# Rotary embedding on unnormalised queries in two sparse mixers, a new step order up to the first combinations, and later weight splits at three stage ends

## The chip, the cores and the metric

The kernel runs on one core of a Trainium2 chip. The metric is the device time of one execution in microseconds (us). All arithmetic is fp32: each large product is made of three TensorE passes over rounded high and low parts (w_hi·x_hi + w_hi·x_lo + w_lo·x_hi), so every weight tile has to be split into a high part (ScalarE, a copy) and a low part (VectorE, a subtraction) before TensorE can use it.

## What is computed

Two blocks of a transformer over 512 tokens and 1024 channels follow each other: four gated feed-forward layers around a retention/dilated mixer and a stick-breaking mixer (`first_block`), then two hybrid layers with a sparse mixer and a squared-ReLU feed-forward layer each (`second_block`). The change is mostly in the sparse mixer of the hybrid layers:

```python
def hybrid_layer(...):
    h = rms_norm_2(x, norm1) * (1.0 + scale1) + shift1
    proj = h @ w_in                      # u (pool), q, kv, gates
    y_pool = pool_mixer(u, pool_w, pool_scale)
    y_nsa = nsa_mixer(q, ..., gates, q_norm, k_norm, ...)
    x = x + gate1 * (jnp.concatenate([y_pool, y_nsa], axis=-1) @ w_out)
    ...                                  # feed-forward

def nsa_mixer(...):
    q = rope(rms_norm_2(q, q_norm), pos)             # 8 heads of 64
    s_c = einsum(q, k_cmp) * scale                   # compressed branch, 31 keys
    p_c = softmax(where(mask_c, s_c, NEG)); o_cmp = p_c @ v_cmp
    s = einsum(q, k_s) * scale; p = softmax(s)       # selected branch
    sw = einsum(q, k_w) * scale; pw = softmax(sw)    # window branch
    o = g0 * o_cmp + g1 * o_s + g2 * o_w
```

rms_norm divides each query head by a root mean square, one number for each token and head. rope is linear in q, so this factor can be applied to q itself or to the scores.

## The kernel before

The activation is kept as x[128, 8, 512]: channels on partitions, tokens along the free dimension. The program has ten stages, F1_0, HYB, F2_0, F1_1, STICK, F2_1, NSA_0, REL_0, NSA_1, REL_1. For each stage a planner (`plan_ffn`, `plan_hyb`, `plan_stick`, `plan_nsa`, `plan_rel`) writes one list of steps, and each of the five engine programs walks the same list in the same order and carries out its own part of each step. So where a step stands in the list sets its place in the queue of every engine that has a part in it. Between engines there are semaphores only (`wait_ge`).

Weights come in units of up to 128x1024 through a ring of four. The step ("load", u) makes ScalarE copy unit u to its high part `wh` (`weights` in `act_program`), makes VectorE subtract to the low part `wl` (`weights` in `dve_program`), and makes SyncE start the DMA of unit u+4 as soon as the low part of unit u has been written. A step that uses unit u is followed by the load of u+3 (AHEAD).

A sparse mixer (`plan_nsa`, stages NSA_0 and NSA_1) runs: normalisation; products for the compression window, the pooled groups 0 to 2, the keys and values; four q units ("q", 0..3: queries with tokens on partitions in PSUM banks 4 to 7); the gates unit; the pooled unit 3. Around them stand small steps:

- "q norm": ScalarE squares the four banks, VectorE sums over heads, ScalarE and VectorE form 1/rms (`root_means`, `norm_root`). It comes behind the gates unit.
- "q evac" t: VectorE multiplies bank 4+t by 1/rms, makes the two halves times sine and the whole times cosine in SBUF, GpSimd adds (semaphore `n_rot`). t = 0 and 1 stand before the pooled unit 3, t = 2 and 3 behind it.
- "turn q" t: TensorE transposes, ScalarE copies to qT.
- "u evac" 3, "u fine" 3, "pool" 3: GpSimd's running sums of the pooled group with window 16 (four doublings), VectorE's subtraction, one product, split into a0h and a0l slot 3.
- "cmp" n (n = 0, 1): scores of the compressed branch (16 small matmuls), mask and softmax on VectorE, ScalarE and GpSimd, all in one VectorE step, with waits for ScalarE and GpSimd inside it.
- "A" c (c = 0..7, a pair of heads and a branch, here called combination c): scores of 24 matmuls; VectorE `low_scores` (8 operations, scale, mask and maximum in one) and ScalarE 8 exponentials. "soft" c: reciprocal and gate on VectorE, eight multiplications on GpSimd. "B" c: 20 transposes of the weights, copied by ScalarE and VectorE. "C" c: product with the values. "pc": transposes of the compressed weights. Between them stand output products of 4 or 2 tiles ("out", with "load" and "add" to x).

In the loop over c (0 to 10) the steps are soft c-1, C c-3, B c-2, pc (only c = 2), outputs, A c. At c = 1, u fine 3, pool 3 and cmp 1 stand behind soft 0; at c = 0 there is A 0 alone, and cmp 0 is ahead of it.

At the end of a mixer stage, output unit d is followed by the add of d-1, the load of d+3 and the square of tile d-1 ("tile"). The loads behind the last three units belong to the next stage, 1024 columns wide. In NSA the next stage begins with a mean over all tiles, which waits for the last add; the transition's own first load comes ahead of it.

```python
for t in range(4):                     # "q norm" in dve_program, before
    dve.wait_ge(*n_sq[s, what, t])
    m = dve.tensor_reduce(v[:, n * t:n * t + n], src, AX.X, ALU.add)
```

## Time and profile before

| | us |
|---|---|
| median of 3 runs | 3204.42 (3203.95 to 3205.21) |
| the profiled execution, its own time | 3201.24 |
| its span, first to last instruction | 3199.4 |
| TensorE busy | 3091.9 |
| VectorE busy | 1673.5 |
| ScalarE busy | 1110.3 |
| GpSimd busy | 677.2 |

TensorE has work for 97% of the span. The mean clock granted to it is 0.981 of full speed. NSA_0 lies at about 2002 to 2235 us of the span, NSA_1 at about 2613 to 2846 us. A line of the profile names the kernel line of a helper (L68 is any matmul, L71 any transpose, L74 any ScalarE activation, L77 tensor_tensor, L80 scalar_tensor_tensor, L97 the scores' operation), so instructions are told apart by their tiles, shapes and order.

### The profile page before, as it was taken

Reading aid. Unit: us, or ns where it says so; the run is one execution under the profiler, and the core shown is the slowest. Engines: PE = TensorE matmul, PEld = TensorE weight load, DVE = VectorE, ACT = ScalarE, POOL = GpSimd, SP = SyncE. Lnnn points to the kernel's source line nnn. Section 1 sums busy time; section 2 is a strip of 40 time slices with the busy share of each in tenths; the row PEclk is TensorE's granted clock in tenths of the full one; section 3 lists DMA queues with packets and bytes.
Section 4 is the critical chain, followed back from the end, with each engine's and each line's share of the span. In section 5 each row is a group of like instructions: output and inputs, shape, how many; then the busy total and the mean of one; then the engine's idle time right before and its main releaser. Section 6 shows DMA issues by size and latency. Waiting matters only on the chain.

```text
span 3199.4 us, 36691 instructions
## 1 busy us (share of the span) xinstructions
PE 3091.9 (97%) x14506; PEld 2504.3 (78%) x14506; DVE 1673.5 (52%) x2485; ACT 1110.3 (35%) x1751; POOL 677.2 (21%) x543
## 2 busy tenths in 40 slices
PE   9999989999999999999999999978999997989999
PEld 7888877788888888877788887756888875768887
DVE  5455556644555454628754555666433356663333
ACT  4222334433223322334332224345422232543321
POOL 2100222111002100144111003255211123632110
PEclk9999999999999999999999999979999997999999
DMA  5344422343443344421243443202332330023332
GB/s 184 116 151 133 127 72 67 94 130 118 154 136 125 113 142 135 131 88 44 64 140 115 156 135 108 70 12 72 92 98 94 99 108 30 18 86 106 99 98 74
DMA packets 115802, 330.49 MB, mean 103 GB/s; under 512 B 13616, under 2 KB 18864, under 8 KB 115248
## 3 DMA queue, kind: packets, MB, share of 16 engines
q1 hardware_dynamic: 115632, 328.15, 32.5%
q8 instruction: 116, 1.90, 0.2%
q14 instruction: 54, 0.44, 0.0%
HBM read 326.00 MB, written 2.10 MB: 103 GB/s over the span
## 4 chain that ended last, share of the span: by engine, by line
PE 88%; DVE 5%; ACT 3%; POOL 2%; issue 1%; DMA 0%; SPq 0%; DVEq 0%; ACTq 0%; POOLq 0%
PE ps L68 87%; ACT s_tmp L74 2%; POOL s_tmp L85 2%; DVE s_tmp L77 1%; PE ps L71 1%; DVE s_wl L77 1%; DVE s_x L80 1%; POOL s_tmp L77 1%; DVE s_small L91 0%; DVE s_hl L80 0%; DVE s_tmp L80 0%; ACT s_hh L74 0%; ACT s_wh L74 0%; DVE s_tmp L100 0%; DVE s_tmp L97 0%
## 5 line engine op out<-in xcount | busy, mean ns | idle before, releaser
L74 ACT ACTIVATE s_wh<-s_raw 128x1024 fp32r<-128x1024 f32 (+3 forms) x562 | 544.5, 970 | 1134.6 <-PE ps L68 1133.5
L68 PE MATMUL ps<-s_hh,s_wh 128*128 128x512 f32 x2320 | 902.6, 394 | 23.4 <-ACT s_hh L74 12.3
L77 DVE TENSOR_TENSOR s_wl<-s_raw,s_wh 128x1024 fp32r<-128x1024 f32 (+3 forms) x535 | 606.8, 1135 | 556.6 <-ACT s_wh L74 556.2
L68 PE MATMUL ps<-s_hh,s_wl 128*128 128x512 f32 x2320 | 895.5, 391 | 0.4 <-DVE s_wl L77 0.3
L68 PE MATMUL ps<-s_hl,s_wh 128*128 128x512 f32 x2320 | 894.0, 390 | 0.2
L77 POOL TENSOR_TENSOR s_tmp<-s_tmp 128x512 f32<-128x512 f32 (+2 forms) x236 | 305.2, 1297 | 1714.1 <-ACT s_tmp L74 1472.6
L68 PEld LDWEIGHTS ps<-s_hh,s_wh 128*128 128x128 f32 x2320 | 437.4, 189 | 121.8 <-issue 12.0
L68 PEld LDWEIGHTS ps<-s_hl,s_wh 128*128 128x128 f32 x2320 | 437.6, 189 | 94.4 <-DVE s_hl L80 2.3
L68 PEld LDWEIGHTS ps<-s_hh,s_wl 128*128 128x128 f32 x2320 | 438.2, 189 | 93.2 <-DVE s_wl L77 1.8
L68 PE MATMUL ps<-s_a0h,s_wh 128*128 128x512 f32 x960 | 380.1, 396 | 7.4 <-ACT s_tmp L74 5.4
L68 PE MATMUL ps<-s_a0l,s_wh 128*128 128x512 f32 x960 | 376.5, 392 | 0.0
L68 PE MATMUL ps<-s_a0h,s_wl 128*128 128x512 f32 x960 | 376.4, 392 | 0.0
L68 PEld LDWEIGHTS ps<-s_a0h,s_wh 128*128 128x128 f32 x960 | 182.0, 190 | 46.6 <-ACT s_tmp L74 5.9
L68 PEld LDWEIGHTS ps<-s_a0h,s_wl 128*128 128x128 f32 x960 | 181.8, 189 | 38.5
L68 PEld LDWEIGHTS ps<-s_a0l,s_wh 128*128 128x128 f32 x960 | 182.1, 190 | 37.7 <-DVE s_a0l L77 0.3
L68 PE MATMUL ps<-s_a1h,s_wh 128*128 128x512 f32 x512 | 199.2, 389 | 0.0
L68 PE MATMUL ps<-s_a1l,s_wh 128*128 128x512 f32 x512 | 199.2, 389 | 0.0
L68 PE MATMUL ps<-s_a1h,s_wl 128*128 128x512 f32 x512 | 199.2, 389 | 0.0
L80 DVE SCALAR_TENSOR_TENSOR s_x<-ps,s_mod,s_x 128x512 f32<-128x512 f32 (+1 forms) x116 | 84.4, 730 | 202.7 <-PE ps L68 202.6
L74 ACT ACTIVATE s_tmp<-ps 128x512 f32<-128x512 f32 (+6 forms) x250 | 129.4, 546 | 107.8 <-PE ps L71 56.7
L85 POOL TENSOR_SCALAR s_tmp<-s_tmp,s_small 128x512 f32<-128x512 f32 (+3 forms) x128 | 137.7, 1098 | 64.5 <-DVE s_small L77 64.5
L80 DVE SCALAR_TENSOR_TENSOR s_x<-ps,s_x 128x512 f32<-128x512 f32 x129 | 88.2, 685 | 119.4 <-PE ps L68 119.4
(135 smaller groups left out, 2948.4 us busy)
## 6 DMA issues: line engine op xcount, KB each, us to landing
s_raw<-in_ff_dram SPq DMA_DIRECT2D x128, 512.0 KB, 3.6
s_tmp<-in_w_mod_dram SPq DMA_DIRECT2D x192, 256.0 KB, 3.6
s_raw<-in_f1i_dram SPq DMA_DIRECT2D x88, 512.0 KB, 3.6
s_raw<-in_f2i_dram SPq DMA_DIRECT2D x88, 512.0 KB, 3.6
s_raw<-in_f1o_dram SPq DMA_DIRECT2D x32, 512.0 KB, 3.6
s_raw<-in_f2o_dram SPq DMA_DIRECT2D x32, 512.0 KB, 3.6
s_raw<-in_nsa_dram SPq DMA_DIRECT2D x30, 512.0 KB, 3.6
s_raw<-in_hyb_dram SPq DMA_DIRECT2D x28, 512.0 KB, 3.5
```

The source lines that it names most:

```text
L68: return self.eng.matmul(o, w, m, **kw) if self.eng is not None else Blank()
L71: return self.eng.transpose(*a) if self.eng is not None else Blank()
L74: return self.eng.activation(o, a, f, **kw) if self.eng is not None else Blank()
L77: return self.eng.tensor_tensor(o, a, b, f) if self.eng is not None else Blank()
L80: return self.eng.scalar_tensor_tensor(o, a, s, b, f, g) if self.eng is not None else Blank()
L85: return self.eng.tensor_scalar(o, a, s, t, f) if g is None else self.eng.tensor_scalar(o, a, s, t, f, g)
```

## The change

1. `plan_nsa`: behind the fourth q unit come "q squares" and the four "q evac"; then the pooled unit 3 (ahead of the gates unit now, and the weights are laid out in that order); turn q 0 and 1; "q norm"; the gates unit; turn q 2 and 3; split 0; cmp 0; u fine 3; pool 3, all of that before A 0. The second half of the VectorE part of "cmp" n becomes a step of its own, "cmp p" n, at c = n+1. "pc" stands behind the outputs of c = 2.
2. "q evac" reads the raw queries in PSUM: two half products with sine, one with cosine. The product with 1/rms is gone. 1/rms times -0.125 is formed once (one more small operation) and is used as the per-partition scale in `low_scores`, where -0.125 stood. In "cmp" there are two further operations that multiply the scores by it.
3. In the NSA stages, the loads behind the last three output units come after the last add and tile; in HYB and STICK that holds for the last load only.

```diff
@@ plan_hyb and plan_stick
-        steps.append(("load", u + AHEAD))
+        if half == 0 or d < KT - 1:
+            steps.append(("load", u + AHEAD))
...
-    steps += [("add", 1, 7), ("tile", 7)]
+    steps += [("add", 1, 7), ("tile", 7), ("load", len(stream.src) - 1 + AHEAD)]
@@ plan_nsa
-    steps += [("turn kv", 2), ("turn kv", 3)]
+    steps += [("turn kv", 2), ("turn kv", 3), ("q squares",)] + [("q evac", t) for t in range(4)]
+    dense("pooled", 3)
+    steps += [("u evac", 3), ("turn q", 0), ("turn q", 1), ("q norm",)]
     dense("gates")
-    steps += [("gate row",), ("q norm",), ("q evac", 0), ("q evac", 1)]
-    dense("pooled", 3)
-    steps += [("gate turn",), ("u evac", 3), ("q evac", 2), ("q evac", 3)]
-    steps += [("turn q", t) for t in range(4)] + [("split", 0), ("cmp", 0)]
+    steps += [("gate row",), ("turn q", 2), ("turn q", 3), ("gate turn",), ("split", 0), ("cmp", 0), ("u fine", 3),
+              ("pool", 3)]
...
     for c in range(11):
+        if c in (1, 2):
+            steps.append(("cmp p", c - 1))
         if 1 <= c <= 8:
             steps.append(("soft", c - 1))
         if c == 1:
-            steps += [("u fine", 3), ("pool", 3), ("cmp", 1)]
+            steps.append(("cmp", 1))
...
-        if c == 2:
-            steps.append(("pc",))
         outs([halves.pop(0) for _ in range((0, 2, 2, 1, 1, 1, 1, 0, 0, 0, 0)[c])])
         outs([early.pop(0) for _ in range((0, 0, 0, 0, 0, 0, 0, 2, 2, 2, 2)[c])])
+        if c == 2:
+            steps.append(("pc",))
...
-        steps.append(("load", u + AHEAD))
+        if d + AHEAD < KT:
+            steps.append(("load", u + AHEAD))
+        else:
+            late.append(("load", u + AHEAD))
...
-    steps += [("add", KT - 1, 6), ("tile", KT - 1)]
+    steps += [("add", KT - 1, 6), ("tile", KT - 1)] + late
@@ act_program, nsa
+                    elif kind == "q squares":
+                        act.wait_ge(*unit[unit_at[s, "v", 1]])
+                        act.wait_ge(*n_rot[s, "kv", 3])
+                        for t in range(4):
+                            act.activation(S(38 + t), B(4 + t), ACT.Square).then_inc(*n_sq.up((s, "q", t)))
+                    elif kind == "q norm":
+                        norm_root(s, "q")
@@ dve_program, low_scores
-                                                 scale=-0.125, scalar=1e30, op0=ALU.add, op1=ALU.min,
+                                                 scale=scale(t, hd), scalar=1e30, op0=ALU.add, op1=ALU.min,
@@ dve_program, nsa, "q norm"
+                        if what == "q":
+                            dve.wait_ge(*n_new[s, "q", 2])
+                            dve.tensor_scalar(v, v, -0.125, None, ALU.mult).then_inc(*n_new.up((s, "q", 3)))
@@ "q evac"
-                        dve.wait_ge(*n_new[s, "q", 2])
-                        dve.tensor_tensor(n, heads(B(4 + t)), r.unsqueeze(2).to_broadcast([128, 8, 64]),
-                                          ALU.mult).then_inc(*n_nrm.up((s, "q", t)))
+                        q = heads(B(4 + t))
+                        dve.wait_ge(*n_sq[s, "q", t])
...
-                            m = dve.tensor_tensor(sn[:, :, 32 * h:32 * h + 32], n[:, :, 32 - 32 * h:64 - 32 * h], q_table(1, t, h),
-                                                  ALU.mult)
+                            dve.tensor_tensor(sn[:, :, 32 * h:32 * h + 32], q[:, :, 32 - 32 * h:64 - 32 * h], q_table(1, t, h),
+                                              ALU.mult)
-                        dve.tensor_tensor(n, n, q_table(0, t, None), ALU.mult).then_inc(*n_sn.up((s, "q", t)))
+                        dve.tensor_tensor(n, q, q_table(0, t, None), ALU.mult).then_inc(*n_sn.up((s, "q", t)))
@@ "cmp"
+                        for t in range(2):
+                            r = small_at("q", 0)[:, 16 * n + 8 * t:16 * n + 8 * t + 8].rearrange("p (i g) -> p g i", g=2)
+                            m = dve.tensor_tensor(p3[:, 8 * t:8 * t + 8, :].rearrange("p (g i) n -> p g i n", g=2),
+                                                  ps[:, 1, 256 * t:256 * t + 256].rearrange("p (g i n) -> p g i n", g=2, i=4),
+                                                  r.unsqueeze(3).to_broadcast([128, 2, 4, 32]), ALU.mult)
-                            m = dve.scalar_tensor_tensor(p3[:, 8 * t:8 * t + 8, :], B(b).rearrange("p (h n) -> p h n", n=32)[:, 8 * t:8 * t + 8, :],
-                                                         0.125, bc, ALU.mult, ALU.add)
+                            m = dve.scalar_tensor_tensor(p3[:, 8 * t:8 * t + 8, :], p3[:, 8 * t:8 * t + 8, :], -1.0, bc, ALU.mult,
+                                                         ALU.add)
```

## Rows read from the trace of the kernel before

**Rows 1.** The page's first part: busy time, share, instructions of each engine
```profile
PE 3091.9 (97%) x14506; PEld 2504.3 (78%) x14506; DVE 1673.5 (52%) x2485; ACT 1110.3 (35%) x1751; POOL 677.2 (21%) x543
```

**Rows 2.** Windows: start:end length, busy PE PEld DVE ACT POOL, granted clock, DMA share, GB/s
```profile
2061.10:2072.30 11.20, 11.20 (x52) 9.01 (x50) 5.03 (x12) 4.67 (x11) 0.00 (x0) 1.00 0.07 23
2072.30:2128.00 55.70, 30.73 (x156) 24.86 (x155) 36.71 (x83) 18.32 (x50) 23.57 (x25) 0.63 0.04 12
...
2135.30:2204.00 68.70, 65.64 (x480) 46.67 (x480) 43.65 (x143) 42.06 (x129) 52.39 (x49) 1.00 0.06 18
...
2684.00:2739.30 55.30, 30.30 (x154) 24.48 (x152) 36.39 (x83) 18.28 (x50) 23.52 (x25) 0.63 0.04 13
```

**Rows 3.** Windows of PE alone: length, busy PE, granted clock, DMA share, GB/s
```profile
2075.00:2115.00 40.00, 20.56 (x82) 0.50 0.02 7
```

**Rows 4.** Timeline of PE in NSA_0: start, us, operation, [idle before <-releaser]
```profile
2075.55 1.12 PE L71 MATMUL ps<-s_ident,s_tmp 128*128 128x128 f32 x4 [2.86 <-POOL s_tmp L77]
...
2089.81 3.65 PE L68 MATMUL ps<-s_tmp 128*128 128x64 f32 x16 [0.78 <-ACT s_tmp L74]
2093.39 3.89 PE L68 MATMUL ps<-s_tmpr 64*128 64x512 f32 x24
2106.37 5.35 PE L68 MATMUL ps<-s_tmp 128*128 128x512 f32 x18 [9.10 <-DVE s_tmp L80]
...
2127.97 0.50 PE L68 MATMUL ps<-s_a0h,s_wh 128*128 128x512 f32 x1 [2.70 <-ACT s_tmp L74]
2135.26 2.19 PE L68 MATMUL ps<-s_tmpr 64*128 64x512 f32 x24
```

**Rows 5.** Timeline of ACT and of DVE around q norm, q evac, u fine
```profile
2066.93 2.51 ACT L74 ACTIVATE s_tmp<-ps 32x512 f32<-32x512 f32 x5 [4.53 <-PE ps L68]
...
2068.03 2.46 DVE L91 TENSOR_REDUCE s_small<-s_tmp 128x8 f32<-128x512 f32 x4 [4.91 <-ACT s_tmp L74]
...
2072.67 1.49 DVE L77 TENSOR_TENSOR s_tmp<-s_tmp 128x256 f32<-128x256 f32 x3
...
2083.50 3.02 DVE L77 TENSOR_TENSOR s_tmp<-s_tmp 128x256 f32<-128x256 f32 x3
...
2105.14 1.08 DVE L80 SCALAR_TENSOR_TENSOR s_tmp<-s_tmp,s_ssum 128x496 f32<-128x496 f32 x1
```

**Rows 6.** Timeline of POOL: a q add, the u chain's first and last sum, soft 0
```profile
2074.24 1.26 POOL L77 TENSOR_TENSOR s_tmp<-s_tmp 128x512 f32<-128x512 f32 x1 [21.49 <-DVE s_tmp L77]
...
2078.52 1.03 POOL L77 TENSOR_TENSOR s_ssum<-s_ssum 128x511 f32<-128x511 f32 x1
...
2084.18 0.39 POOL L103 COPY s_tmp<-s_ssum 128x8 f32<-128x8 f32 x1
...
2105.01 8.52 POOL L85 TENSOR_SCALAR s_tmp<-s_tmp,s_small 128x512 f32<-128x512 f32 x8 [6.45 <-DVE s_small L77]
```

**Rows 7.** Groups of DVE by form, whole span: count | busy us, mean ns | idle before
```profile
L80 DVE SCALAR_TENSOR_TENSOR s_x<-ps,s_x 128x512 f32<-128x512 f32 x127 | 87.5, 689 | 117.7 <-PE ps L68 117.7
L80 DVE SCALAR_TENSOR_TENSOR s_x<-ps,s_mod,s_x 128x512 f32<-128x512 f32 x108 | 80.9, 749 | 195.0 <-PE ps L68 194.9
L97 DVE CUSTOM_DVE_ANT_0 s_tmp<-ps,s_tmp 128x512 f32<-128x512 f32 x40 | 26.0, 686 | 4.0 <-PE ps L68 3.8
```

**Rows 8.** Timeline at the end of NSA_0: DVE, ACT, PE
```profile
2223.10 1.66 DVE L77 TENSOR_TENSOR s_wl<-s_raw,s_wh 128x1024 fp32r<-128x1024 f32 x1
...
2228.11 1.04 ACT L74 ACTIVATE s_wh<-s_raw 128x1024 fp32r<-128x1024 f32 x1
2232.00 0.47 ACT L74 ACTIVATE s_tmp<-ps,s_eps 128x256 f32<-128x256 f32 x1 [2.85 <-PE ps L68]
...
2227.90 1.51 PE L68 MATMUL ps<-s_ssum,s_ones 128*128 128x256 f32 x4 [4.20 <-DVE s_x L80]
```

**Rows 9.** Timeline at the end of HYB: DVE, PE
```profile
637.04 1.21 DVE L77 TENSOR_TENSOR s_wl<-s_raw,s_wh 128x1024 fp32r<-128x1024 f32 x1
...
639.57 0.50 PE L68 MATMUL ps<-s_hh,s_wh 128*128 128x512 f32 x1 [1.92 <-DVE s_x L80]
```

More of the change, by code:

```diff
@@ L288, in out @@
             steps.append(("add",) + add)
-        steps.append(("load", u + AHEAD))
+        if half == 0 or d < KT - 1:
+            steps.append(("load", u + AHEAD))
         if half and d:
@@ L320, in plan_stick @@
         out(1, d, (1, d - 1) if d else None)
-    steps += [("add", 1, 7), ("tile", 7)]
+    steps += [("add", 1, 7), ("tile", 7), ("load", len(stream.src) - 1 + AHEAD)]
     return steps
@@ L384, in plan_nsa @@
             steps.append(("B", c - 2))
+        outs([halves.pop(0) for _ in range((0, 2, 2, 1, 1, 1, 1, 0, 0, 0, 0)[c])])
+        outs([early.pop(0) for _ in range((0, 0, 0, 0, 0, 0, 0, 2, 2, 2, 2)[c])])
         if c == 2:
             steps.append(("pc",))
-        outs([halves.pop(0) for _ in range((0, 2, 2, 1, 1, 1, 1, 0, 0, 0, 0)[c])])
-        outs([early.pop(0) for _ in range((0, 0, 0, 0, 0, 0, 0, 2, 2, 2, 2)[c])])
         if c < 8:
@@ L392, in plan_nsa @@
                 steps.append(("split", c // 2 + 1))
+    late = []
     for d in range(KT):
@@ L397, in plan_nsa @@
             steps.append(("add", d - 1, 6))
-        steps.append(("load", u + AHEAD))
+        if d + AHEAD < KT:
+            steps.append(("load", u + AHEAD))
+        else:
+            late.append(("load", u + AHEAD))
         if d:
             steps.append(("tile", d - 1))
-    steps += [("add", KT - 1, 6), ("tile", KT - 1)]
+    steps += [("add", KT - 1, 6), ("tile", KT - 1)] + late
     assert not halves and not early
@@ L1096, in nsa @@
                             for t in range(4):
-                                free[b0 + t] = [(n_nrm, (s, kind, t))] + ([(v_up, (s, 0, t))] if kind == "kv" else [])
+                                if kind == "kv":
+                                    free[b0 + t] = [(n_nrm, (s, "kv", t)), (v_up, (s, 0, t))]
+                                else:
+                                    free[b0 + t] = [(n_sn, (s, "q", t)), (n_sq, (s, "q", t))]
                     elif kind == "gates":
@@ L1535, in nsa @@
                         tile(s + 1, step[1])
-                    elif kind in ("kv norm", "q norm"):
-                        what = kind[:-5]
-                        act.wait_ge(*unit[unit_at[s, "v", int(what == "q")]])
+                    elif kind == "kv norm":
+                        act.wait_ge(*unit[unit_at[s, "v", 0]])
                         act.wait_ge(*win_add[s, 1, 1])
-                        n, b0, o = (256, 0, 0) if what == "kv" else (512, 4, 4)
                         for t in range(4):
-                            if what == "q" and t == 0:
-                                act.wait_ge(*h_lo[s, 7])
-                            dst = tmp[:, 42 + t, 0:n] if what == "kv" else S(46 + t)
-                            act.activation(dst, ps[:, b0 + t, 0:n], ACT.Square).then_inc(*n_sq.up((s, what, t)))
-                            if what == "kv":
-                                act.activation(vsw[:, t, :], ps[:, t, 256:512], ACT.Copy).then_inc(*v_up.up((s, 0, t)))
-                        norm_root(s, what)
+                            act.activation(tmp[:, 42 + t, 0:256], ps[:, t, 0:256], ACT.Square).then_inc(*n_sq.up((s, "kv", t)))
+                            act.activation(vsw[:, t, :], ps[:, t, 256:512], ACT.Copy).then_inc(*v_up.up((s, 0, t)))
+                        norm_root(s, "kv")
+                    elif kind == "q squares":
[5 more added lines that the diff above has]
+                        norm_root(s, "q")
                     elif kind == "turn kv":
@@ L1805, in mix_lo, with low_scores @@
                 dve.tensor_tensor(a0l[:, slot, :], src, f32(a0h[:, slot, :]), ALU.subtract).then_inc(*a_lo.up((s, 0, slot)))
-            def low_scores(s, i, g, z, st, bs, bias):
+            def low_scores(s, i, g, z, st, bs, bias, scale):
                 dve.wait_ge(*score[s, i, g])
@@ L1865, in hyb @@
                         for g in range(3):
-                            low_scores(s, i, g, Z[s][0], i % 2, ((6, 7), (4, 5), (2, 3))[g], DIL_BIAS)
+                            low_scores(s, i, g, Z[s][0], i % 2, ((6, 7), (4, 5), (2, 3))[g], DIL_BIAS,
+                                       lambda t, hd: -0.125)
                     elif kind == "soft":
@@ L2061, in nsa @@
                         for t in range(4):
-                            src = kv_tmp(t)[0] if what == "kv" else q_tmp(t)[0]
+                            src = kv_tmp(t)[0] if what == "kv" else heads(S(38 + t))
                             n = src.shape[1]
@@ L2197, in nsa @@
                         dve.tensor_tensor(p3, p3, mx.unsqueeze(2).to_broadcast([128, 16, 32]), ALU.subtract).then_inc(
-                            *cmp_low.up((s, n, 1)))
+                            *cmp_low.up((s, n, 2)))
+                    elif kind == "cmp p":
+                        n = step[1]
+                        p3 = S(36 + n).rearrange("p (h n) -> p h n", n=32)
+                        dn = small[:, 14 + n, :]
                         dve.wait_ge(*cmp_ex[s, n])
@@ L2434, in nsa @@
                             pool.tensor_copy(to[:, 0:sh], cur[:, 0:sh]).then_inc(*u_sum.up((s, g, n) if n < g else (s, g)))
-                    elif kind == "cmp":
+                    elif kind == "cmp p":
                         n = step[1]
```

28 lines of the change are left out of this document (14 added, 14 removed).

## The prediction

> **What bounds the kernel now.** I read the page first. TensorE is busy 3091.9 of 3199.4 us [rows 1], so all that can be won is its 107.5 us of idle time and what it loses at a low clock. Then I read the windows along the span. In NSA_0 the 55.7 us behind the pooled unit 3 hold only 30.7 us of TensorE work at a mean clock of 0.63; NSA_1 has the same hole, 55.3 us with 30.3 [rows 2]. The hole is 25 us of idle time plus a clock loss: from 2075 to 2115 the granted clock is 0.50 (1.2 GHz), with 20.56 us busy that would be 10.3 at 2.4 GHz [rows 3]. From 2135.3 to 2204 TensorE is busy 65.6 of 68.7 us at full clock [rows 2], so there is next to nothing to win there. Third I read the TensorE timeline for what it waits on. Turn q 0 waits 2.86 us for a GpSimd add, that is, for the q norm and evacuation; cmp 0 starts only at 2089.81; behind A 0 it stands 9.10 us until u fine 3 is done, which is queued behind the whole of cmp 0 and soft 0 on VectorE; the first outputs of c = 2 wait 2.70 us for ScalarE's pc copies; A 2 starts at 2135.26 [rows 4]. So the bound in this hole is a serial chain through VectorE, ScalarE and GpSimd: squares, sums, root, evacuation, turn, cmp, softmax, u fine.
>
> **The change, middle of a mixer (twice).** I take the fixed point "q unit 3 done" at 2061.1 and walk to the start of A 2, from which the loop is as before.
>
> TensorE: pooled 3 and gates are 52 records in 11.2 us [rows 2], 5.6 each. Pooled 3 runs to 2066.7. Turn q 0 and 1 take 0.4 each (1.12 for one at half clock [rows 4], half of that plus overlap), gates run to 2073.1.
>
> Squares: four of 0.5 us on ScalarE [rows 5], now from 2061.9, behind the key copies. Evacuation: the three products of one tile took 1.49 us [rows 5] and now read PSUM; the fourth is gone. Four tiles: 5.8 us, 2062.5 to 2068.3; before it was 2072 to 2086.5, because GpSimd's sums ran beside it (3.02 instead of 1.49 for three products [rows 5]). The adds take 1.26 us each [rows 6] and end at about 2069.6. Turns 0 and 1 need adds 0 and 1 (2065.1, 2066.5): ready. Turns 2 and 3 are ready behind the gates. ScalarE then has gate row and two copies of q, 0.5 each: cmp 0 starts at about 2074.9 instead of 2089.81. This is the part with one answer: 14.9 us earlier.
>
> The norm itself (VectorE sums 2.46 us [rows 5], root about 1.4, one more small operation 0.2) now lies beside the gates unit, 2069.2 to 2073.5. Its cover ends with cmp 0 at 2076.7 (3.65 at half clock [rows 4], so 1.85). Bound: 2073.3 if nothing is in its way, 2076 if its two-input operations stand behind GpSimd's u chain, which takes 6.0 us (2078.52 to 2084.57 [rows 6]) and now runs 2069.6 to 2075.6.
>
> In that place the trace shows: three evacuation products beside the u chain took 3.02 us, alone 1.49 [rows 5]. The Trainium skill has the rule for it ("SBUF — State Buffer", section on who interferes with whom): a VectorE instruction with two SBUF inputs and a GpSimd instruction that reads SBUF exclude each other for a whole instruction, one with at most one SBUF input does not. It speaks for the new evacuation (one input in PSUM) and against the new cmp, whose mask operation moves from PSUM to two SBUF inputs; by it, cmp 1 beside GpSimd's soft 0 could lose up to one GpSimd instruction for each such operation. The sum below goes by rows in either case.
>
> VectorE then does a low-part split, the gate reciprocal, split 0 (to about 2078), cmp 0 (an operation over 512 columns takes about 0.7 [rows 7]; mask, maximum and subtraction were three, now there are four, 2.9), and u fine 3, 1.08 [rows 5] and two small ones, 1.3 us: to about 2082.2. Bounds 2081.1 without contention and 2083. **Here is the new wait**: pool 3 stands ahead of A 0 in TensorE's queue and waits for u fine 3, with A 0, cmp 1 and the outputs queued behind it. TensorE idles 2076.7 to 2082.2. Idle times of 2.86 and 2.70 us were followed by a clock of 0.50 [rows 3, 4], so I take half clock: pool 3 1.7 (5.35 less 3.65), A 0 3.9, cmp 1 3.65 [rows 4] to 2091.4. Before, the clock was still low at 2115 [rows 3], 8.6 us into the busy stretch that began at 2106.37 [rows 4], and full behind it, so here at about 2091; the two outputs take 5.5 (24 matmuls at 0.227), A 1 2.1: TensorE is at 2099.0.
>
> VectorE meanwhile: scores of A 0 to 2088.6; cmp p 0, 2.9 with GpSimd's mask inside, to 2091.5; soft 0; cmp 1, 2.9 to 4, to 2095; two splits and two adds, 3.6, to 2098.6; scores of A 1, 2560 columns at 0.686 for 512 [rows 7], 3.4, and 0.5 more as follows, to 2102.7. The scale by pointer is not in the trace. Nearest rows: the add with a pointer scale takes 749 ns, with an immediate one 689 [rows 7]; 0.06 each, 0.5 for eight, between 0 and 0.12; it is in the 2102.7. GpSimd's soft 0, 8.5 us [rows 6] from 2092, gives its last half at 2100.7. B 0 needs the banks of A 1's scores, so it ends at about 2103.2. Outputs of c = 2: 5.5 us, and 0.7 for half a chance of another low clock like that behind 2127.97; pc is behind them, 0.9. A 2 starts at 2110.3 instead of 2135.26 [rows 4]: **25.0 us a mixer, 50.0 in all**. Bounds: every contention absent and full clock throughout, 2107.3 (28 us); all contention, and the low clock until 2100, 2116 (19 us). The loop behind has 3 us idle of 68.7 and keeps its order, so nothing is late next there: 0.
>
> **The change, stage ends.** NSA: VectorE has 1024-wide splits between the last adds (1.66 us with GpSimd's sums beside it), the mean starts at 2227.90, 0.14 behind the last add, and TensorE stood 4.20 us before it [rows 8]. So the last product ends at 2223.7, so the add is done at 2224.5 without the splits and the mean starts 3.25 us earlier. But ScalarE has three more copies of 1.04 [rows 8] ahead of the root, besides the one of the next stage: from 2225.3 four of 0.97 to 2229.2. The root starts there instead of at 2232.00 [rows 8], 2.8 earlier; VectorE's fourth split ends at 2230.4, so the first scaled tile is 2.5 earlier. I take 2.5, twice: 5.0. The DMAs of the following units wait on SyncE for these splits and start some 4 us later; the units are needed 20 us after. Bounds per end: 1, if root or split is later still; 3.5, if the clock stays up.
>
> HYB: TensorE waits 1.92 us for the last adds; the split of 1.21 between them goes behind [rows 9]: 1.1 (0 to 1.2). ScalarE has copied already. STICK: TensorE has no wait in that transition, the edit costs and gives nothing; its cover is the next layer's first two products, 11 us at the rate of rows 2.
>
> **Sum.** 50.0 + 5.0 + 1.1 = 56.1 us. Against the profiled execution, 3201.24, that is 3145.1; it was 3.2 us (0.1%) below the median, and the gain is the same for both, so the median of 3204.4 goes to **3148.3**.
>
> **The rivals.**
> (a) *Full clock and short waits.* The norm meets no u chain, the wait for u fine is 4 us, and the clock is up again at once. 28 + 3.3 a stage: 3204.4 - 62.6 - 1.1 = 3140.7. For it: most new operations read PSUM. Against: every idle time near 3 us in the hole brought the low clock.
> (b) *Later in the chain.* Contention on VectorE, pool 3's wait near 6.5 us, low clock to 2100. 19 + 1.5 a stage: 3204.4 - 41.0 - 0.5 = 3162.9. For it: 40 us on end at 0.50 in rows 3 although TensorE was busy 7.5 us in a row there, from 2089.81 [rows 4].
> (c) *Only the front moves.* From cmp 0 to A 2 lie 45.5 us [rows 4]; if the reordered steps there gain nothing (pool 3's wait takes the place of the 9.10, VectorE's new cmp operations that of its old waits), 14.9 a mixer stays: 3204.4 - 29.8 - 5.5 = 3169.1. This is also the case in which the change doesn't do what its new order says.
> (d) *The other side.* The pointer scale makes the scores' operation slow. 64 of them in a mixer stand in the loop, 8 a combination of about 10 us, of which VectorE is busy 64% [rows 2]. Up to 0.4 us each it is hidden; beyond, VectorE is the bound, and each further 0.1 costs 12.8 us in all. At 0.9 us extra each: 3204.4 - 56.1 + 64 = 3212. Against: the pair in rows 7.
>
> **How the numbers follow.** Forecast 3148.3, chance 0.52 for 3143 to 3157; (a) 0.15; (b) 0.17; (c) 0.08; within 0.2% of no change 0.03, if several of them meet; (d) or another loss 0.05. The range takes in (a) and (b): 3138 to 3165. A measurement can tell 0.2% (6.4 us) from no change. Faster by more: 0.92; same 0.03; slower 0.05.
>
> **What would show it.** Turn q 0 without a wait; cmp 0 near 2075; one idle time of 4 to 6 us ahead of pool 3, released by u fine; cmp 0 to A 2 35 us; the window of the hole (pooled 3's end to the outputs of c = 2) near 30 us instead of 55.7; at the end of NSA the 4.20 gone to about 1 and the first scaled tile 2.5 earlier; HYB's 1.92 down to 0.8; L97 at 512 columns near 750 ns. The forecast is wrong if GpSimd's soft 0 rather than VectorE ends B 0 late, if the norm ends behind cmp 0, or if the loop behind A 2 gets longer than 68.7 us.

## The result and the profile after

The changed kernel takes 3153.03 us (median, 3151.05 to 3157.45); the kernel before, beside it on the same chip, 3204.18. The ratio is 0.9847 (95% interval 0.9836 to 0.9859): 51.2 us saved, against 56.1 forecast. Its profiled execution is its longest one: 3157.45 us with a span of 3155.6.

The page's first part, as in [rows 1]. TensorE's busy time fell by 10.2 us (the same 14506 instructions, fewer of them at the low clock), its idle time from 107.5 to 73.9 us:

```profile
PE 3081.7 (98%) x14506; PEld 2495.5 (79%) x14506; DVE 1669.3 (53%) x2487; ACT 1109.2 (35%) x1751; POOL 671.8 (21%) x543
```

Windows of the changed kernel, columns as in [rows 2]: the two units behind turn kv 3 (pooled 3 and gates), then the hole up to the outputs of c = 2, then the loop from A 2 to the last product, in NSA_0 and, last line, in NSA_1:

```profile
2062.90:2074.90 12.00, 12.00 (x60) 9.94 (x59) 10.66 (x21) 5.69 (x13) 8.85 (x10) 1.00 0.06 22
2074.90:2105.80 30.90, 23.04 (x140) 18.55 (x138) 23.56 (x66) 14.26 (x43) 11.81 (x14) 0.79 0.07 22
2113.70:2201.80 88.10, 85.71 (x573) 61.90 (x572) 60.12 (x165) 52.81 (x149) 62.79 (x60) 1.00 0.14 45
...
2699.70:2793.20 93.50, 90.24 (x574) 64.09 (x572) 59.57 (x165) 52.95 (x149) 63.96 (x60) 0.95 0.13 43
```

The hole is 30.9 us instead of the 55.7 of [rows 2], its mean clock 0.79 instead of 0.63. The loop has the same waits as before, but in this execution NSA_1 spent part of it at a low clock (0.95 on average, 93.5 us for 88.1).

TensorE's timeline in NSA_0, to be read against [rows 4]. Pooled 3 starts at 2062.94, which is the prediction's fixed point (2061.1 in the kernel before):

```profile
2062.94 0.48 PE L68 MATMUL ps<-s_hh,s_wh 128*128 128x512 f32 x1
...
2068.51 1.03 PE L71 MATMUL ps<-s_ident,s_tmp 128*128 128x128 f32 x8
...
2074.88 1.40 PE L71 MATMUL ps<-s_ident,s_tmp 128*128 128x128 f32 x12
2076.81 2.00 PE L68 MATMUL ps<-s_tmp 128*128 128x64 f32 x16 [0.53 <-ACT s_gate_s L74]
2082.86 2.04 PE L68 MATMUL ps<-s_tmp 128*128 128x512 f32 x2 [4.06 <-DVE s_tmp L80]
2084.84 3.89 PE L68 MATMUL ps<-s_tmpr 64*128 64x512 f32 x24
2088.66 2.31 PE L68 MATMUL ps<-s_tmp 128*128 128x64 f32 x16
2090.78 0.48 PE L68 MATMUL ps<-s_a0h,s_wh 128*128 128x512 f32 x1
...
2096.42 1.79 PE L68 MATMUL ps<-s_tmpr 64*128 64x512 f32 x18
2100.56 0.62 PE L68 MATMUL ps<-s_tmpr 64*128 64x256 f32 x6 [2.35 <-DVE s_x L80]
2101.32 1.24 PE L71 MATMUL ps<-s_ident,s_tmp 128*128 128x128 f32 x8
2103.34 2.79 PE L71 MATMUL ps<-s_ident,s_tmp 128*128 128x128 f32 x12 [0.78 <-DVE s_small L97]
2105.78 0.77 PE L68 MATMUL ps<-s_a0h,s_wh 128*128 128x512 f32 x1
...
2112.67 1.10 PE L71 MATMUL ps<-s_ident,s_tmp 128*128 128x128 f32 x8 [0.86 <-DVE s_x L80]
2113.70 2.20 PE L68 MATMUL ps<-s_tmpr 64*128 64x512 f32 x24
```

The four turns of q wait for nothing. cmp 0 starts 13.9 us behind the fixed point, A 2 (2113.70) 50.8 behind it instead of 74.1; in NSA_1 it is 50.7 (2649.00 to 2699.74) instead of 73.9. The waits 2.86, 9.10 and 2.70 of [rows 4] are gone, the 0.78 ahead of cmp 0 is 0.53, and three new ones stand there: 4.06 ahead of pool 3, 2.35 ahead of A 1's last group, 0.86 ahead of pc. The first was forecast; the other two weren't.

The end of NSA_0 in the changed kernel (DVE, ACT and PE), against [rows 8]. The mean waits 1.06 us instead of 4.20, the four splits lie behind the last add, and the root comes behind ScalarE's four copies:

```profile
2204.12 4.63 DVE L77 TENSOR_TENSOR s_wl<-s_raw,s_wh 128x1024 fp32r<-128x1024 f32 x4 [1.43 <-ACT s_wh L74]
...
2203.05 3.88 ACT L74 ACTIVATE s_wh<-s_raw 128x1024 fp32r<-128x1024 f32 x4
2206.84 0.45 ACT L74 ACTIVATE s_tmp<-ps,s_eps 128x256 f32<-128x256 f32 x1
...
2202.84 1.10 PE L68 MATMUL ps<-s_ssum,s_ones 128*128 128x256 f32 x4 [1.06 <-DVE s_x L80]
2203.78 1.89 PE L68 MATMUL ps<-s_tmp,s_ones 128*128 128x256 f32 x8
2210.33 2.07 PE L68 MATMUL ps<-s_hh,s_wh 128*128 128x512 f32 x4 [4.66 <-ACT s_hh L74]
```

The last product ends at 2201.78 (2202.84 less 1.06), so 8.55 us lie between it and the first scaled tile's product; before they were 11.18 (2223.70 to 2234.88). In NSA_1 it is 8.54 for 11.19.

### The profile page after: what moved, and what is told of

It is laid out like the page before. It is cut to its first block, busy times and chain, and to the rows that moved or that the text cites. A ratio compares the mean times of both kernels' runs of the same rounds, so it can differ in the third digit from the quotient of the medians.

```text
span 3155.6 us, 36691 instructions
## 1 busy us (share of the span) xinstructions
PE 3081.7 (98%) x14506; PEld 2495.5 (79%) x14506; DVE 1669.3 (53%) x2487; ACT 1109.2 (35%) x1751; POOL 671.8 (21%) x543
## 4 chain that ended last, share of the span: by engine, by line
PE 90%; DVE 4%; ACT 3%; POOL 2%; issue 1%; DMA 0%; DVEq 0%; SPq 0%; ACTq 0%; POOLq 0%
PE ps L68 88%; POOL s_tmp L85 2%; ACT s_tmp L74 2%; PE ps L71 1%; DVE s_tmp L77 1%; DVE s_wl L77 1%; DVE s_x L80 0%; DVE s_tmp L97 0%; POOL s_tmp L77 0%; ACT s_hh L74 0%; ACT s_wh L74 0%; DVE s_tmp L80 0%; DVE s_tmp L100 0%; DVE s_hl L80 0%; DVE s_small L91 0%
## 5 line engine op out<-in xcount | busy, mean ns | idle before, releaser
L74 ACT ACTIVATE s_tmp<-ps 128x512 f32<-128x512 f32 (+7 forms) x250 | 129.3, 547 | 85.2 <-PE ps L71 41.6
L77 DVE TENSOR_TENSOR s_a0l<-s_tmp,s_a0h 128x512 fp32r<-128x512 f32 x88 | 60.9, 692 | 171.0 <-ACT s_a0h L74 171.0
```

The lines of the kernel that those rows point to most:

```text
L74: return self.eng.activation(o, a, f, **kw) if self.eng is not None else Blank()
L77: return self.eng.tensor_tensor(o, a, b, f) if self.eng is not None else Blank()
```

## Where the 51 us come from

| part | forecast | measured in the profiles |
|---|---|---|
| middle of the mixers, fixed point to A 2 | 2 x 25.0 | 23.35 + 23.2 |
| ends of the NSA stages | 2 x 2.5 | 2.63 + 2.65 |
| end of HYB | 1.1 | 0.27 |
| end of STICK | 0 | 0 |
| sum | 56.1 | 52.1 |

The two spans differ by 43.8 only. In this execution 5.2 us went to the low clock in NSA_1's loop, 1.6 to one in STICK (both below). The remaining 1.5 lie in the stretches between these places, and no run says what they are.

## Experiments

Stretches are from the fixed point (0.36 us behind the start of turn kv 3's transposes in each trace) to A 2, first in NSA_0 and then in NSA_1. The experiments were measured in three groups, on three chips, each with the kernel before beside it: 3202.74 us for the first four below, 3203.45 for the next four and 3202.21 for the last four. Across groups, compare what a kernel saves against its own kernel before; the changed kernel saves 51.2 and, in the second group, 51.8.

**Late loads alone.** The kernel before with only part 3 of the change.

```diff
-        steps.append(("load", u + AHEAD))
+        if half == 0 or d < KT - 1:
+            steps.append(("load", u + AHEAD))
...
-    steps += [("add", KT - 1, 6), ("tile", KT - 1)]
+    steps += [("add", KT - 1, 6), ("tile", KT - 1)] + late
```

> The kernel before with nothing but the late loads of the stage ends (HYB, STICK and both sparse mixers). Theory: the late loads bring 2.6 us at each sparse mixer's end and little elsewhere, since in HYB the split stood in a time in which VectorE would have waited for ScalarE's h_hi anyway; 2 x 2.6 + 0.3 = 5.5 us, so about 3198.7, and from the last product to the first scaled tile's product 8.55 us instead of 11.18 in both mixers. Rival 1 (the prediction's term): HYB gives 1.1, 3197.9. Rival 2: STICK's late load costs 1.5 us (the trace of the changed kernel loses 1.6 us in that transition): 3200.2, with the loss visible in STICK's last 50 us. At HYB's end the first theory wants a wait ahead of the ones product of about 1.7 us, rival 1 of 0.8.

Measured: 3198.20 us for 3202.74, ratio 0.9985 (0.9976 to 0.9994), 4.5 us. The total can't choose between 5.5 and 6.3, but the wait does: 1.66 us of it are left at HYB's end, for 1.92. (It stands ahead of the next layer's first product, the line of [rows 9], and not ahead of the ones product, as the expectation has it.) At the ends of NSA_0 and NSA_1 8.55 us lie between the last product and the first scaled tile's. The theory holds; the 1.1 of the prediction doesn't.

**HYB's and STICK's last load back in its old place**, in the changed kernel (the first hunk above undone).

> The changed kernel with HYB's and STICK's last load back in its old place; the sparse mixers keep theirs. Theory: HYB's edit is worth 0.3 us and STICK's nothing, the 1.6 us lost in STICK in the profile of the changed kernel is a fall of the granted clock after a wait that both kernels have (1.96 before, 1.91 after): 3153.3, the same as the changed kernel. Rival: the late load in STICK costs 1.5: 3151.8. Rival 2: HYB's edit is worth the 1.1 of the prediction: 3154.1. Local: HYB's ones product with 1.9 us of wait in each case.

Measured: 3155.89 us, ratio 0.9854 (0.984 to 0.9867), inside the interval of the changed kernel. It saves 46.9, some 4 less, which this edit doesn't account for: both stretches are 50.8, as in the changed kernel. What does decide is local: HYB's wait is 1.93 again, so the edit is worth 0.27 there. Why so little shows in the changed kernel's VectorE timeline at the end of HYB, to be read against [rows 9]:

```profile
637.05 0.68 DVE L80 SCALAR_TENSOR_TENSOR s_x<-ps,s_x 128x512 f32<-128x512 f32 x1
638.52 0.75 DVE L80 SCALAR_TENSOR_TENSOR s_hl<-s_x,s_gains,s_hh 128x512 fp32r<-128x512 f32 x1 [0.79 <-ACT s_hh L74]
639.19 0.68 DVE L80 SCALAR_TENSOR_TENSOR s_x<-ps,s_x 128x512 f32<-128x512 f32 x1
```

Between the last two adds stands a low part for the next stage's tile 6, and that waits 0.79 us for ScalarE. The split of 1.21 us had lain over that wait.

For STICK, one pair of windows (columns as in [rows 2]) settles it. TensorE waits for the last add ahead of the second half of the outputs in every trace: 1.96 us in the kernel before, 1.91 in the changed one. The changed kernel, behind that wait:

```profile
1571.00:1573.00 2.00, 2.00 (x6) 1.60 (x5) 1.32 (x3) 0.00 (x0) 0.00 (x0) 0.50 0.63 176
1573.00:1575.00 2.00, 2.00 (x8) 1.55 (x8) 0.36 (x1) 0.30 (x1) 0.00 (x0) 0.77 0.43 133
```

and the late loads alone, which have the same STICK:

```profile
1571.00:1573.00 2.00, 1.63 (x7) 1.35 (x8) 2.00 (x4) 0.00 (x0) 0.00 (x0) 1.00 0.43 131
1573.00:1575.00 2.00, 2.00 (x11) 1.62 (x10) 1.25 (x3) 0.47 (x1) 0.00 (x0) 1.00 0.59 151
```

The first ran at 1.2 GHz for about 3 us, the second at 2.4 throughout. From the end of that wait to the mean's product at STICK's end it is 48.44 us in the kernel before, 48.44 with the late load and no fall of the clock, and 50.06 here, with the load in its old place and a fall. The changed kernel itself has 50.01 with the fall and, in a second profile (below), 48.40 without. So the 1.6 us belong to the clock and not to the edit.

**Fixed scale.** The changed kernel with the old immediate in the scores' operation, which leaves 1/rms out of two branches.

```diff
-                                       lambda t, hd: r[:, 8 * t + 2 * (c // 2) + hd:8 * t + 2 * (c // 2) + hd + 1])
+                                       lambda t, hd: -0.125)
```

> The changed kernel with the fixed factor -0.125 in the scores' operation in place of the pointer to 1/rms. This leaves 1/rms out of the selected and window branches, so the output is another one. Theory: the pointer costs 0.06 us for each of the 8 operations of a combination; only combinations 0 and 1 lie on the chain, so 0.5 to 1 us a mixer: 3151.5, the stretch from the end of turn kv 3 to A 2 50.0 us instead of 50.75. Rival: the pointer scale is what the stretch is longer than predicted by (1.7 us a mixer): 3149.6, stretch 49.1. Second rival: it costs in all eight combinations, 64 x 0.06 = 3.8 a mixer: 3145.4, the loop from A 2 on 85 instead of 88.

Measured: 3151.46 us, ratio 0.984 (0.9827 to 0.9854). The stretch is 50.2 and 50.1 us instead of 50.8 and 50.7. The theory's 0.5 a mixer holds, and the total can't tell it from nothing. The groups of DVE by form in the changed kernel, columns as in [rows 7], give the 0.06 us for each operation (746 for 686):

```profile
L97 DVE CUSTOM_DVE_ANT_0 s_tmp<-ps,s_tmp,s_small 128x512 f32<-128x512 f32 x32 | 22.7, 746 | 4.2 <-PE ps L68 4.2
...
L97 DVE CUSTOM_DVE_ANT_0 s_tmp<-ps,s_tmp 128x512 f32<-128x512 f32 x8 | 5.2, 686 | 2.0 <-PE ps L68 1.8
```

**New order, but normalised before rope.** The scores and cmp have fixed factors again, and cmp loses its two extra operations.

```diff
-    steps += [("turn kv", 2), ("turn kv", 3), ("q squares",)] + [("q evac", t) for t in range(4)]
+    steps += [("turn kv", 2), ("turn kv", 3), ("q squares",), ("q norm",)] + [("q evac", t) for t in range(4)]
...
+                        dve.tensor_tensor(n, heads(B(4 + t)), r.unsqueeze(2).to_broadcast([128, 8, 64]),
+                                          ALU.mult).then_inc(*n_nrm.up((s, "q", t)))
```

> The changed kernel's step order, but the queries are normalised before rope: q norm stands right behind the squares, ahead of the evacuation, which has its four operations again, and the scores and cmp have fixed factors. Theory: raw rope is worth 3 to 4 us a mixer: sums 2.5, root 1.4 and four more operations of 0.7 stand ahead of turn q 3, which ends about 7 us later, of which the gates unit hides some 3; cmp 0 starts 17.5 us behind the end of turn kv 3 instead of 13.9, GpSimd's sums for the pooled unit follow later too, pool 3 starts at about 23.5 instead of 19.9: 3160. Rival: the order does all of it, raw rope is hidden by the gates unit: 3153. Other rival: raw rope is the main part, 10 us a mixer: 3173.

Measured: 3166.78 us, ratio 0.9891 (0.9877 to 0.9904); the stretch is 57.3 and 56.5. That is between theory and the other rival: 6.2 a mixer. TensorE's timeline shows turns 0 and 1 holding up the gates unit behind them, which I hadn't counted; the next kernel shows that this is only 0.6 of the 6.2:

```profile
2072.33 0.66 PE L71 MATMUL ps<-s_ident,s_tmp 128*128 128x128 f32 x4 [3.04 <-POOL s_tmp L77]
2075.02 1.12 PE L71 MATMUL ps<-s_ident,s_tmp 128*128 128x128 f32 x4 [2.03 <-POOL s_tmp L77]
...
2085.51 2.00 PE L68 MATMUL ps<-s_tmp 128*128 128x64 f32 x16 [0.53 <-ACT s_gate_s L74]
```

**The same with turns 0 and 1 behind the gates unit.**

```diff
-    steps += [("u evac", 3), ("turn q", 0), ("turn q", 1)]
+    steps += [("u evac", 3)]
...
-    steps += [("gate row",), ("turn q", 2), ("turn q", 3), ("gate turn",), ("split", 0), ("cmp", 0), ("u fine", 3),
+    steps += [("gate row",), ("turn q", 0), ("turn q", 1), ("turn q", 2), ("turn q", 3), ("gate turn",), ("split", 0), ("cmp", 0), ("u fine", 3),
```

> As the kernel that normalises before rope in the new order, but with turns q 0 and 1 behind the gates unit, so that the gates unit isn't held up by them (there they waited 3.04 and 2.03 us). Theory: raw rope proper is worth the later end of turn q 3 and of GpSimd's sums, 4.4 us a mixer: cmp 0 18.4 behind the end of turn kv 3 (now 13.9, in the other 21.7), pool 3 24.3 behind it: 3162. Rival 1: the place of the turns changes nothing since GpSimd's sums, queued behind the adds, set the time of pool 3: 3167. Rival 2: with the turns late the gates unit hides all: 3154.

Measured: 3162.31 us, against 3151.68 for the changed kernel in the same group; the stretch is 56.3 twice. cmp 0 starts at 2081.49, 19.3 behind the fixed point (2062.22), pool 3 at 2088.42, 26.2 behind it: each later than I had said (18.4 and 24.3). The turns ahead of cmp 0 wait 2.03 and 2.41, and cmp 0 behind them takes 3.67 us at the low clock. In the new order raw rope is worth 5.6 us a mixer, and the new order without it 17.8 (74.1 less 56.3). What raw rope would bring in the old order was not run.

**The changed kernel once more.**

> The changed kernel once more, as the yardstick of this group and for its own profile. Theory: the 1.6 us lost in STICK and the 5.2 us lost in NSA_1's loop in the first profile are falls of the granted clock that come in some executions and not in others; so here one or both are absent or lie elsewhere, with every wait the same to 0.1 us: 3153, span 3149 to 3156. Rival: they are set by the new order, so the second profile shows the same loss in NSA_1's loop (93.4 us from A 2 to the last product instead of 88.1).

Measured: 3151.68 us, ratio 0.9839 (0.9824 to 0.9854), span of the profiled execution 3147.9. A window of this second profile, NSA_1 from A 2 to the last product, against the last line of the windows above:

```profile
2698.00:2786.00 88.00, 85.66 (x573) 61.91 (x572) 60.10 (x165) 52.78 (x149) 62.65 (x60) 1.00 0.14 45
```

88.0 us at full clock where the first profile had 93.5 at 0.95. The stretches are 50.6 and 50.75, as before. The loss in the loop is of the execution and not of the order of steps. The same would account for the 6.4 us between the four runs of the changed kernel: the two fastest have a mean granted clock of 0.991, the next 0.990, the slowest 0.989.

**u fine 3 and pool 3 back behind soft 0.**

```diff
-    steps += [("gate row",), ("turn q", 2), ("turn q", 3), ("gate turn",), ("split", 0), ("cmp", 0), ("u fine", 3),
-              ("pool", 3)]
+    steps += [("gate row",), ("turn q", 2), ("turn q", 3), ("gate turn",), ("split", 0), ("cmp", 0)]
...
         if c == 1:
-            steps.append(("cmp", 1))
+            steps += [("u fine", 3), ("pool", 3), ("cmp", 1)]
```

> The changed kernel with u fine 3 and pool 3 back in their old place, behind cmp p 0 and soft 0 and ahead of cmp 1. Theory: A 0 then follows cmp 0 at once, but u fine 3 stands behind the scores of A 0 and cmp p 0 on VectorE, and pool 3, cmp 1 and the outputs wait for it: pool 3 some 7 us later than now, the outputs 3 to 4 later, A 2 2 to 3 later: 3158. Rival: VectorE's queue from cmp 0 to the scores of A 1 is the bound and its sum is the same in either order, so A 2 doesn't move: 3153.

Measured: 3161.54 us, ratio 0.987 (0.9854 to 0.9887); the stretch is 55.1 and 55.0. Direction right, size too small: 4.3 a mixer instead of 2 to 3. TensorE:

```profile
2089.03 5.35 PE L68 MATMUL ps<-s_tmp 128*128 128x512 f32 x18 [9.33 <-DVE s_tmp L80]
```

That is the 9.10 of [rows 4] back again, and the granted clock is 0.50 from 2085 to 2095 (full from 2100), which I hadn't counted.

**pool 3 behind A 0.** u fine 3 stays where it is on VectorE.

```diff
-    steps += [("gate row",), ("turn q", 2), ("turn q", 3), ("gate turn",), ("split", 0), ("cmp", 0), ("u fine", 3),
-              ("pool", 3)]
+    steps += [("gate row",), ("turn q", 2), ("turn q", 3), ("gate turn",), ("split", 0), ("cmp", 0), ("u fine", 3)]
...
             steps.append(("A", c))
+            if c == 0:
+                steps.append(("pool", 3))
```

> The changed kernel with pool 3 alone (TensorE's product and its two copies) moved behind A 0; u fine 3 stays ahead of the scores of A 0 on VectorE. Theory: the 4.06 us ahead of pool 3 were a wait that A 0 need not share. A 0 runs at 2079 to 2082, VectorE takes its scores from 2082.7 and goes on without a gap, its queue up to the scores of A 1 ends 3.5 us earlier (2100.7 for 2104.2), pool 3 waits 1 to 2 us for u fine 3 and nothing else does: A 2 47.3 behind the end of turn kv 3 instead of 50.75, 3146. Rival 1: the clock stays low in that stretch and takes back half: 3150. Rival 2: the queue of VectorE is filled by its own waits for ScalarE and GpSimd, nothing is gained: 3153.

Measured: 3147.80 us, ratio 0.9826 (0.9812 to 0.9841), 3.9 less than the changed kernel beside it; the stretch is 49.4 twice. That is 1.3 a mixer where the theory said 3.5. VectorE's timeline names what took the rest:

```profile
2088.62 0.75 DVE L80 SCALAR_TENSOR_TENSOR s_a0l<-ps,s_nsm,s_a0h 128x512 fp32r<-128x512 f32 x1 [2.01 <-ACT s_a0h L74]
...
2096.71 0.69 DVE L77 TENSOR_TENSOR s_wl<-s_raw,s_wh 128x512 fp32r<-128x512 f32 x1 [1.22 <-ACT s_wh L74]
...
2105.05 0.69 DVE L77 TENSOR_TENSOR s_tmpr<-s_tmp,s_tmpr 128x512 fp32r<-128x512 f32 x1 [1.96 <-ACT s_tmpr L74]
```

Pool 3's high part now stands behind A 0's eight exponentials on ScalarE, and VectorE waits for it with everything else in its queue behind. Three waits for ScalarE, each a place where another VectorE step could lie. The next three kernels shorten them one after the other.

**Low part of pool 3 inside cmp p 0.**

```diff
                     elif kind == "pool":
                         g = step[1]
+                        if g == 3:
+                            continue
...
                     elif kind == "cmp p":
...
+                        if n == 0:
+                            dve.wait_ge(*a_hi[s, 0, 3])
+                            dve.scalar_tensor_tensor(a0l[:, 3, :], B(POOL_BANK[3]), pscale[:, 3:4], f32(a0h[:, 3, :]), ALU.mult,
+                                                     ALU.subtract).then_inc(*a_lo.up((s, 0, 3)))
```

> The kernel with pool 3 behind A 0, and VectorE's part of pool 3 (the low part a0l) moved again, into cmp p 0, where VectorE stands 0.76 us waiting for GpSimd's mask. Theory: pool 3 behind A 0 brought 1.2 us a mixer instead of 3.5 because its a0l stood 2.01 us on VectorE, waiting for ScalarE's a0h, which ScalarE writes behind the 8 exponentials of A 0; with the wait hidden the scores of A 1 and A 2 come 2.0 earlier: 3147.8 - 4.0 = 3143.8, A 2 47.4 behind the end of turn kv 3 instead of 49.44. Rival: the next wait of VectorE (1.22 for the high part of the unit, 1.96 for split 1) or pc's wait for the add takes it: 3147.

Measured: 3151.89 us, ratio 0.984 (0.9827 to 0.9854); the stretch is 49.3 and 48.6. The rival is right about the stretch, 0.2 and 0.8 shorter. The kernel before had 3147.80 and 0.9826 (0.9812 to 0.9841) in another group; the intervals overlap, so it isn't shown that this one is slower, only that nothing was gained. VectorE's timeline at the second add of c = 1:

```profile
2097.40 0.75 DVE L80 SCALAR_TENSOR_TENSOR s_x<-ps,s_mod,s_x 128x512 f32<-128x512 f32 x1 [1.67 <-PE ps L68]
```

TensorE's timeline, pc and A 2:

```profile
2110.68 1.09 PE L71 MATMUL ps<-s_ident,s_tmp 128*128 128x128 f32 x8 [2.36 <-DVE s_x L80]
2111.70 3.74 PE L68 MATMUL ps<-s_tmpr 64*128 64x512 f32 x24
```

The wait for a0h is down from 2.01 to 0.58, but VectorE is early and waits 1.67 us for the outputs of c = 1. And A 2 takes 3.74 us for the 2.19 of [rows 4], at 1.2 GHz (granted clock 0.50 from 2112 to 2114); the loop lasts 90.2 and 89.6 instead of 88.1 and 88.3. The profiled execution takes 1.6 us more than that of the kernel before; the medians, each against its own kernel before, save 5.3 less. Why the clock falls there in this kernel and not in the one before, behind the same wait of 2.36, stays open.

**cmp p 1 ahead of split 1**, on top of that.

```diff
-        if c in (1, 2):
-            steps.append(("cmp p", c - 1))
+        if c == 1:
+            steps.append(("cmp p", 0))
...
             steps.append(("A", c))
...
+            if c == 1:
+                steps.append(("cmp p", 1))
             if c % 2 == 1 and c < 7:
                 steps.append(("split", c // 2 + 1))
```

> As the one before, with cmp p 1 ahead of split 1, in the 1.96 us in which VectorE waits for ScalarE's high part of split 1. Theory: pc waits for the add on bank 0, that add stands behind cmp p 1, soft 1 and the copies of B 0, so the chain is VectorE's queue; filling the 1.96 brings pc and A 2 forward by 1.9 a mixer, until the end of the outputs of c = 2 is the bound: A 2 45.5 behind the end of turn kv 3, 3140. Rival: TensorE's own queue (B 0 and the outputs) is the bound by then, 0.5 a mixer: 3143.

Measured: 3143.57 us, ratio 0.9813 (0.98 to 0.9827); the stretch is 46.1 and 46.9. 8.3 us less than the kernel before it in the same group: in the two profiles 4.9 in the stretches and 2.8 in the loops behind A 2, which last 88.6 and 88.3 again. Against pool 3 behind A 0, the stretches are 3.4 and 2.6 shorter, while the totals save 58.6 for 55.7 with intervals that overlap. pc's wait for the add falls from 2.36 to 0.32: VectorE's queue was what set A 2.

**First load of c = 1 ahead of cmp 1**, on top of that.

```diff
-            steps.append(("load", u + AHEAD))
+            if these[n] != (0, 0, 4):
+                steps.append(("load", u + AHEAD))
...
-            steps.append(("cmp", 1))
+            steps += [("load", len(stream.src) + AHEAD), ("cmp", 1)]
```

> As the one before, with the first load of c = 1 ahead of cmp 1, so that ScalarE's copy of it doesn't stand behind cmp 1's exponential. Theory: VectorE's wait of 1.22 there falls to 0.5, 0.6 us a mixer: 3138.8. Rival: what is saved is waited for at B 0 (GpSimd's soft 0, 8.84 us): 3140.

Measured: 3141.58 us (3139.34 to 3144.04), ratio 0.981 (0.9796 to 0.9823); the stretch is 46.0 twice. It can't be told from the one before it. But it is faster than the changed kernel: 60.6 us below its kernel before, where that one was 51.2 and 51.8, and the intervals of the ratios don't overlap.

**Banks of the outputs swapped** in the changed kernel.

```diff
-                        bank_of[u] = (0, 7)[n % 2] if k < 6 else (0, 2, 3, 4, 5)[n % 5]
+                        bank_of[u] = (7, 0)[n % 2] if k < 6 else (0, 2, 3, 4, 5)[n % 5]
```

> The changed kernel with the two PSUM banks of the output units swapped (7 first, then 0). A 1's third group then waits for the first add of c = 1 instead of the second, pc for the second add of c = 2 instead of the first. Theory: A 1's wait (2.35 to 3.65 us) is beside the chain, since VectorE takes that group's scores last anyway; pc's wait is on it. So A 1's wait falls by 1.3, pc's grows by 1.3, A 2 is 1.3 later in each mixer: 3155. Rival: A 1's wait is on the chain and pc's replaces it: 3152, no change. Other rival: the long wait before A 1's third group is what brings the low clock in B 0, and with it gone the outputs are faster: 3150.

Measured: 3154.01 us, ratio 0.9848 (0.9835 to 0.9862); the stretch is 52.0 twice, 1.3 longer, exactly the theory. The total can't show it: 48.2 saved for 51.2 and 51.8, with intervals that overlap. TensorE:

```profile
2099.85 0.62 PE L68 MATMUL ps<-s_tmpr 64*128 64x256 f32 x6 [1.27 <-DVE s_x L80]
...
2114.50 1.09 PE L71 MATMUL ps<-s_ident,s_tmp 128*128 128x128 f32 x8 [1.75 <-DVE s_x L80]
```

A 1's wait fell from 2.35 to 1.27 and A 2 came later all the same: the long new wait lies beside the chain, the short one, pc's, on it. The last rival is out too: B 0 and the outputs behind it still ran at a mean clock of 0.69 from 2104 to 2110.

## Why the prediction was right, and where not

- *The front.* cmp 0 13.9 us behind the fixed point, forecast 13.8. Evacuation 1.3 us a tile, forecast 1.45. Turns without a wait, as said. This part carries 14.8 of the 23.3 us.
- *The norm beside the gates unit.* It ended at 2076.65, 13.7 behind the fixed point: halfway between the value taken (12.4) and the late bound (14.9). VectorE and then GpSimd of the changed kernel show the contention as whole instructions:

```profile
2072.70 1.03 DVE L85 TENSOR_SCALAR s_small<-s_small 128x32 f32<-128x32 f32 x1
2074.29 0.69 DVE L77 TENSOR_TENSOR s_small<-s_small 128x32 f32<-128x32 f32 x1 [0.56 <-ACT s_small L74]
2075.02 1.42 DVE L80 SCALAR_TENSOR_TENSOR s_small<-s_small 128x32 f32<-128x32 f32 x2
2076.47 0.18 DVE L85 TENSOR_SCALAR s_small<-s_small 128x32 f32<-128x32 f32 x1
...
2072.65 1.04 POOL L77 TENSOR_TENSOR s_tmp<-s_ssum 128x510 f32<-128x510 f32 x1
...
2073.90 1.03 POOL L77 TENSOR_TENSOR s_ssum<-s_tmp 128x508 f32<-128x508 f32 x1
...
2075.14 1.25 POOL L77 TENSOR_TENSOR s_tmp<-s_ssum 128x504 f32<-128x504 f32 x1
```

  The first operation takes 1.03 us beside a sum of 1.04, and the like operation 0.18 once GpSimd's last sum is through (2076.39); the pair of 1.42 took 0.42 in the kernel before, where GpSimd was idle. It cost nothing, but only just: VectorE's queue reached cmp 0 at 2078.70, and TensorE's scores for it were there at about 2078.8.

  The Trainium skill's "SBUF — State Buffer" (who interferes with whom) says that a VectorE instruction with two SBUF inputs, or a scalar operation in a mode with two ports, and a GpSimd instruction that reads SBUF exclude each other. The operations beside the sums agree with it; the prediction had named the first kind only, and whether the operation of 1.03 ran in a mode with two ports no run shows. The evacuation, with one input in PSUM, kept its 1.3 us a tile beside GpSimd's adds. But what the prediction drew from the rule for cmp 1 beside soft 0 didn't come: its mask operations, both inputs in SBUF, take 0.76 in cmp 0, with GpSimd idle, and 0.76 in cmp 1, while GpSimd multiplies from 2093.87 to 2102.71:

```profile
2079.63 0.76 DVE L80 SCALAR_TENSOR_TENSOR s_tmp<-s_tmp 128x256 f32<-128x256 f32 x2
...
2094.47 0.76 DVE L80 SCALAR_TENSOR_TENSOR s_tmp<-s_tmp 128x256 f32<-128x256 f32 x2
...
2093.87 8.84 POOL L85 TENSOR_SCALAR s_tmp<-s_tmp,s_small 128x512 f32<-128x512 f32 x8 [1.22 <-DVE s_small L77]
```

  So beside GpSimd's sums VectorE lost time, beside its multiplications by a scalar it lost none; why they differ is open.
- *The new wait.* Foreseen ahead of pool 3, released by u fine 3, 4 to 6 us: 4.06. The low clock was foreseen too; it ended at about 2089, 4 us sooner behind the fixed point than I had taken. Two errors cancel here, which is luck: pool 3 started 19.9 behind the fixed point instead of 21.1, but VectorE then stood 2.95 us until ScalarE had written a0h, which the prediction doesn't have, and the scores of A 0 were done 27.6 behind it, for 27.5.
- *cmp 0 to A 2.* 36.9 us for 35.4, and this is the step that was mis-sized. Up to the scores of A 1 VectorE's queue was right (done 41.3 behind the fixed point, forecast 41.6, where its own terms add up to 0.2 less). From there the prediction let TensorE's own queue set A 2: B 0, the outputs of c = 2, and "pc is behind them, 0.9", pc's own duration, without asking what its bank waits for. The bank is freed by the first add of c = 2, which VectorE starts 48.9 behind the fixed point in both mixers, since its queue there holds 1.96 us of waiting for ScalarE (split 1), cmp p 1, soft 1 and the copies of B 0. So pc waits 0.86 in NSA_0 and 2.02 in NSA_1:

```profile
2698.72 1.09 PE L71 MATMUL ps<-s_ident,s_tmp 128*128 128x128 f32 x8 [2.02 <-DVE s_x L80]
```

  The low clock of B 0 is not what was missing. In NSA_0 B 0's second part fell under it (2.79 us, 1.50 at full clock with pool 3 behind A 0), and the outputs began 42.8 behind the fixed point, 0.7 later than forecast. In NSA_1 they began at 2690.98, 42.0 behind it; pc's wait took up the difference, and A 2 stood at 50.8 and 50.7. The swap of the banks and cmp p 1 ahead of split 1 both moved A 2 through that wait.
- *NSA ends.* 2.63 and 2.65 for 2.5, with the mechanism as said (root behind the copies).
- *HYB.* 0.27 for 1.1. The sentence that failed is "ScalarE has copied already": that held for the unit's high part, not for the tile's.
- *STICK.* 0, as said.
- *Pointer scale.* 0.06 each, as said; rival (d) is out.
- *The loop behind A 2.* No new wait, as said. But in the first profile it got 5.2 us longer in NSA_1 by the clock alone, so its length isn't the sign that I had named it to be.
- *The rivals.* (a), full clock at once, is out: the granted clock was 0.50 from about 2079 to 2089. (b) put the end of the low clock and A 2 too late. (c), only the front moves, is out: 8.5 us a mixer came behind cmp 0.
